# Halves of the memory in other tiles, made beside the last query columns

## The reference

```python
qkv = u @ w_qkv                                  # 16 query heads, 4 key/value heads of 64
q, k, v = split(qkv); q, k = rotary(q), rotary(k)
# each block of 128 rows looks at itself and the block before it, with a sink:
s = where(valid, (q @ k.T) * 64**-0.5, -inf)
p = exp(s - m); o = (p @ v) / (sum(p) + exp(sink - m))
u = o @ w_o
h = h + rms_norm(u, g_mix_post)
# cross attention to a memory of 256 rows, 4 heads of 256:
q = rms_norm(h, g_x_pre) @ w_q
k, v = split(rms_norm(mem, g_mem) @ w_kv)
u = softmax(q @ k.T / 16) @ v @ w_o
```

## Time and profile before

| | |
|---|---|
| median of 3 runs | 3600.88 us (3600.04 to 3605.23) |
| profiled execution | 3602.97 us, its span 3601.2 us |
| PE busy | 3408.3 us (95%) |
| DVE busy | 1788.2 us (50%) |
| ACT busy | 1326.3 us (37%) |
| mean granted TensorE clock | 0.971 of 2.4 GHz |

### The profile page before, as it was taken

One profiled execution on the slowest core, in us unless ns is written; L12 is line 12 of the kernel. 1 busy time (PEld: TensorE's weight loads), 2 busy tenths in 40 slices (PEclk: granted clock), 3 DMA queues, 4 the chain that ended last, 5 costly groups with the idle time before them and its releaser, 6 DMA issues.

```text
span 3601.2 us, 38290 instructions
## 1 busy us (share of the span) xinstructions
PE 3408.3 (95%) x15668; PEld 2798.7 (78%) x15668; DVE 1788.2 (50%) x2679; ACT 1326.3 (37%) x2104; POOL 112.4 (3%) x100
## 2 busy tenths in 40 slices
PE   8999989999999999899999999898999889889998
PEld 6888777888788887778887778667888678667886
DVE  4333685433453347753334764546444764554444
ACT  3222554322232226543223443334332564334321
POOL 0000000000000000000001000000000100000000
PEclk9999999999999999999999999999999999999999
DMA  4332311333233332123332323212333223113332
GB/s 145 100 100 88 76 47 53 106 97 96 82 94 99 99 95 59 42 76 108 97 97 73 88 83 105 70 42 85 95 98 98 60 59 106 53 42 102 97 98 66
DMA packets 604286, 304.10 MB, mean 84 GB/s; under 512 B 43600, under 2 KB 601808, under 8 KB 603984
## 3 DMA queue, kind: packets, MB, share of 16 engines
q1 hardware_dynamic: 604112, 301.66, 29.2%
HBM read 299.52 MB, written 2.10 MB: 84 GB/s over the span
## 4 chain that ended last, share of the span: by engine, by line
PE 80%; DVE 11%; ACT 6%; issue 1%; DMA 1%; SPq 0%; DVEq 0%; ACTq 0%
PE ps L1561 25%; PE ps L1562 24%; PE ps L1569 24%; DVE XR L2044 2%; DVE wl L1948 1%; PE ps L1578 1%; DVE Y L2121 1%; PE ps L1585 1%; PE ps L1718 1%; PE ps L1619 1%; ACT XH L1775 1%; ACT wh L1733 1%; DVE XL L2030 1%; ACT tmp L1795 1%; PE ps L1604 1%
## 5 line engine op out<-in xcount | busy, mean ns | idle before, releaser
L1561 PE MATMUL ps<-XH,wh 128*128 128x512 f32 x2600 | 1056.1, 406 | 78.9 <-ACT XH L1775 33.1
L1569 PE MATMUL ps<-XL,wh 128*128 128x512 f32 (+1 forms) x2856 | 1067.7, 385 | 0.0
L1562 PE MATMUL ps<-XH,wl 128*128 128x512 f32 x2600 | 1028.4, 396 | 0.0
L1948 DVE TENSOR_TENSOR wl<-raw,wh 128x1024 fp32r<-128x1024 f32 (+1 forms) x565 | 680.4, 1210 | 521.3 <-ACT wh L1733 521.1
L1733 ACT ACTIVATE wh<-raw 128x1024 fp32r<-128x1024 f32 (+1 forms) x565 | 583.3, 1039 | 519.4 <-PE ps L1569 492.6
L1561 PEld LDWEIGHTS ps<-XH,wh 128*128 128x128 f32 x2600 | 499.0, 192 | 200.8 <-issue 36.0
L1569 PEld LDWEIGHTS ps<-XL,wh 128*128 128x128 f32 x2856 | 545.4, 191 | 107.3
L1562 PEld LDWEIGHTS ps<-XH,wl 128*128 128x128 f32 x2600 | 499.8, 192 | 103.6 <-issue 2.7
L1561 PE MATMUL ps<-HHa,wh 128*128 128x512 f32 x1088 | 427.0, 392 | 9.2 <-DVE HLa L1952 5.8
L1562 PE MATMUL ps<-HHa,wl 128*128 128x512 f32 x1088 | 423.6, 389 | 0.0
L1569 PE MATMUL ps<-HLa,wh 128*128 128x512 f32 x1088 | 408.0, 389 | 0.0
(11 more groups left out here) (311 smaller groups left out, 3184.5 us busy)
## 6 DMA issues: line engine op xcount, KB each, us to landing
raw<-in_ffn_w_gu SPq DMA_DIRECT2D x176, 512.0 KB, 3.8
raw<-in_w_ff SPq DMA_DIRECT2D x128, 512.0 KB, 4.1
raw<-in_ffn_w_down SPq DMA_DIRECT2D x64, 512.0 KB, 3.9
raw<-in_w_xkv SPq DMA_DIRECT2D x32, 512.0 KB, 3.9
raw<-in_ev_w_in SPq DMA_DIRECT2D x25, 512.0 KB, 3.9
raw<-in_ffn_w_down SPq DMA_DIRECT2D x32, 384.0 KB, 3.4
raw<-in_w_in SPq DMA_DIRECT2D x24, 512.0 KB, 3.9
raw<-in_w_out SPq DMA_DIRECT2D x64, 128.0 KB, 2.7
```

What stands on the lines that cost most here:

```text
L1561: e.matmul(bank[:, 0:n], t.wh[u % SPL][:, k, :], h, start=first, stop=False)
L1562: e.matmul(bank[:, 0:n], t.wl[u % SPL][:, k, :], h, start=False, stop=False)
L1569: m = e.matmul(bank[:, 0:n], t.wh[u % SPL][:, k, :], l, start=False, stop=last)
L1948: self.e.tensor_tensor(wl, raw, f32(wh), ALU.subtract).then_inc(self.s["lo"], self.tag("lo", f"lo.{i}"))
```

## The change

In the second layer of the second block, the memory's halves leave XL. The hi parts go to Y[6], Y[7], HLb[6] and HLb[7] (two of 256 columns in each), which were lent as temporaries before; the lo parts are written over the raw memory in Y[0:4], through a second view of Y in the rounded type, `Yr`. They no longer wait for query 7's last matmul. `normed` and `parts` become one sequence of 17 steps, four of which are issued after each of queries 4 to 7 and the last one behind them; it takes no attention steps along. `swa` lends two tiles in place of six. The tiles of the halves are given on after the last matmul of the memory (`mem.last`) in place of the last subtraction. For the first layer the halves stay in XL and their order is as it was.

```diff
         self.XL = sb("XL", [P, KD, T], F32R)
+        with nc.sbuf_tensor("Yr", [P, KD, T], F32R) as Yr:
+            self.Yr = Yr
         self.Y = sb("Y", [P, KD, T])
...
-        extra = [Y[:, i, :] for i in range(4, 8)] + [M1[:, i, :] for i in (6, 7)]
-        self.lend(extra[:4], yf)
-        self.lend(extra[4:], menter)
-        mem = Memory(self, 1, Y[:, 0:4, :], yf)
+        extra = [Y[:, i, :] for i in (4, 5)]
+        self.lend(extra, yf)
+        mem = Memory(self, 1, Y[:, 0:4, :], [t.Yr[:, 6, :], t.Yr[:, 7, :], t.HLb[:, 6, :], t.HLb[:, 7, :]], (yf, menter))
+        prep = itertools.chain(mem.normed(), mem.parts())
...
         for i in range(4, 8):
             query(i)
-            if i == 4:
-                for _ in mem.normed():
-                    pass
-        for _ in mem.parts():
-            next(self.filler[0], None)
+            for _ in range(4):
+                next(prep, None)
+        for _ in prep:
+            pass
         for i in range(16):
             mem.unit(i)
 
         def finish():
             mem.turn()
             keys = self.reclaim(extra)
-            self.y_free = [self.y_free, keys, mem.raw_done]
-            self.m_leave(done[0], keys)
+            self.y_free = [self.y_free, keys, mem.last]
+            self.m_leave(done[0], keys, mem.last)
...
-    def __init__(self, walk, l, raw, *free):
+    def __init__(self, walk, l, raw, his, free):
...
-        XL = walk.t.XL
-        self.mh = XL[:, 0:4, :].rearrange("p a (b t) -> p (a b) t", b=2)
-        self.ml = XL[:, 4:8, :].rearrange("p a (b t) -> p (a b) t", b=2)
+        XL, w = walk.t.XL, T // 2
+        if his:
+            self.his = [his[k // 2][:, w * (k % 2):w * (k % 2) + w] for k in range(KD)]
+            self.los = [walk.t.Yr[:, k // 2, w * (k % 2):w * (k % 2) + w] for k in range(KD)]
+            self.free = free
+        else:
+            self.his = [XL[:, k // 2, w * (k % 2):w * (k % 2) + w] for k in range(KD)]
+            self.los = [XL[:, 4 + k // 2, w * (k % 2):w * (k % 2) + w] for k in range(KD)]
+            self.free = None
...
-                w.p_mem_hi(f"{self.k}.h{k}", self.mh[:, k, :], self.tile(k), (f"{self.k}.n{k}", w.x_free))
+                free = w.x_free if self.free is None else self.free
+                w.p_mem_hi(f"{self.k}.h{k}", self.his[k], self.tile(k), (f"{self.k}.n{k}", free))
```

More of the change, by code:

```diff
@@ L1 @@
+import itertools
 import math
@@ L1074, in mixer2 @@
         self.tmp.give(rx, lru_state[3])
-        mem = Memory(self, 0, t.XM[:, 4:8, :], self.x_free)
+        mem = Memory(self, 0, t.XM[:, 4:8, :], None, self.x_free)
         extra = [Y[:, i, :] for i in (0, 1, 4, 5)]
@@ L1431, in parts @@
             if k < KD:
-                w.p_mem_hi(f"{self.k}.h{k}", self.mh[:, k, :], self.tile(k), (f"{self.k}.n{k}", w.x_free))
+                free = w.x_free if self.free is None else self.free
+                w.p_mem_hi(f"{self.k}.h{k}", self.his[k], self.tile(k), (f"{self.k}.n{k}", free))
             if k:
                 j = k - 1
-                w.p_mem_lo(f"{self.k}.l{j}", self.ml[:, j, :], self.tile(j), self.mh[:, j, :], f"{self.k}.h{j}")
-                self.ms.append((self.mh[:, j, :], self.ml[:, j, :], f"{self.k}.l{j}"))
+                w.p_mem_lo(f"{self.k}.l{j}", self.los[j], self.tile(j), self.his[j], f"{self.k}.h{j}")
+                self.ms.append((self.his[j], self.los[j], f"{self.k}.l{j}"))
             yield
```

## The result

The changed kernel takes 3607.02 us (median of 20 runs, 3604.02 to 3609.18); the kernel before takes 3601.62 beside it (20 runs). The ratio is 1.0015, with a 95% interval of 1.0008 to 1.0022. It is slower by 5.4 us: within the 0.2% that the prediction called no change, but above its range, whose upper end was 3605.0, and on the other side of zero from the forecast of -2.0. All lines of the changed kernel lie 11 further down than before (L1952 is L1963 now). The page of the profiled execution (3607.99 us) answers to the earlier trace rows: PE has the same instructions, is busy 1.3 us less in a span 5.0 us longer, and so stands idle 6.3 us more.

What follows compares the result with a forecast made beforehand. PE, busy 95% of the span, was taken as the bound, with an ACT-DVE ring under the query columns. Terms -20.5 + 8.3 + 1.1 + 5.7 + 2.0 + 1.4 = -2.0 us gave 3598.9 us, range 3590.5 to 3605.

Steps and rivals of the forecast that it cites:

- nine attention steps: Steps from the removed stretch come later in PE's queue, at 0.92 us each among units: +8.3 us.
- stretch: PE's time between query 7's last transposes and unit 0's first matmul is removed: -20.5 us.
- normed tiles: Eight DVE operations, four now behind query 4's rotary and four behind query 5's, give and take the same 1.6 us: 0.
- three subtractions on the ring: DVE subtractions behind query 6's rotary, in the ACT-DVE ring of waits under the query columns, delay query 7's end: +1.1 us.
- wait in unit 0: PE waits after unit 0's first matmuls for subtraction 3, issued only after query 7's rotary: +5.7 us, bounds 0 and 7.4.
- half clock behind it: After the wait in unit 0, PE runs at half clock for 4 us: +2.0 us, bounds 0 and 2.9.
- last half: Out projection's k = 7 waits for tile 7's second half, made from step 72 directly ahead: +1.4 us, bounds 0 and 2.
- The sign by which it should show: In the changed kernel's profile, query 7's 0.33 us wait of PE becomes about 1.4 us.
- Full cover: Halves all there when unit 0 begins, no wait or half clock: -9.7 us, 3591.2 us; chance 0.18 including most of it.
- Too few temporaries: Tiles given too late make each of eight projected columns wait like the 1.41 us: +11.3, 3610 us; chance 0.14.

Runs made afterwards that it cites:

- e9: Changed kernel with one attention step issued between query 7 and unit 0; 3598.6 us, ratio to the kernel before 0.9990.
- e6: Changed kernel, memory's 16 DVE operations dealt ahead of rotaries of queries 1 to 7, 8 ACT copies behind those of queries 4 and 5; 3599.8 us.
- e7: e6 with one attention step issued between query 7 and unit 0; 3588.9 us (5 runs), ratio to the kernel before 0.9969.
- e5: Changed kernel with four attention steps issued between query 7 and unit 0; 3602.3 us, ratio to the kernel before 1.0001.
- e3: Changed kernel with all 17 preparing steps dealt 6, 6, 5, 0 behind queries 4 to 7; 3603.1 us, ratio to the kernel before 1.0008.
- e11: e7 repeated unchanged; 3591.3 us (6 runs), ratio to the kernel before 0.9968.
- e10: Changed kernel with three attention steps issued between query 7 and unit 0; 3599.0 us, ratio to the kernel before 0.9989.
- e2: Kernel before, with two lent temporaries in place of six and nothing else; 3601.5 us, ratio to the kernel before 1.0004.
- e1: Changed kernel, with units 10, 12 and 14 taking the second free PSUM bank; 3606.1 us, ratio to the kernel before 1.0017.
- e4: Changed kernel with five attention steps issued between query 7 and unit 0; 3602.6 us, ratio to the kernel before 1.0007.
- e8: e6 with three attention steps issued between query 7 and unit 0; 3594.0 us, ratio to the kernel before 0.9980.

## Why the prediction was wrong

**The step that failed** is "Its nine attention steps are not removed. They come later in PE's queue, beside other work." I priced them as nine pieces of PE time and took their order against the units as without effect. The term for them is +8.3. Moving an odd number of steps across unit 0 turned the parity of every step behind it, and with it two things: the order in which ACT and DVE get a head's split and the next unit's weight halves, and which columns take a bank that a split releases. The price is the four waits, 1.44 + 1.63 + 1.50 + 1.37 = 5.9 us. e9 shows that the odd step makes or removes them on the changed kernel, e6 against e7 on another one, and e5 has the waits back at two places. The two effects of the parity were not tested apart. The timelines above show the first (the split ends 4.9 in place of 3.6 us behind the values), and e9's remaining waits for a split, 0.36 us at most, fit it; the share of the second stays open.

**Point by point**, forecast and measured:

| term | forecast | measured |
|---|---|---|
| stretch | -20.5 | -20.8 |
| nine steps, without waits | +8.3 | about +10.5 |
| normed tiles | 0 | 0 |
| three subtractions on the ring | +1.1 | +1.1 |
| wait in unit 0 | +5.7 | +5.7 |
| half clock behind it | +2.0 | +2.0 |
| last half | +1.4 | +1.5 |
| banks released by a split | none | +5.9 |
| at the first scores, other phase of the clock | none | +1.5 |
| sum over the changed stretch | -2.0 | +7.5 |

- *Nine steps.* The units and the out projection take 117.0 us before and 142.6 after (2938.70 to 3055.69, 2921.05 to 3063.68): +25.6, of which 5.7 + 2.0 + 5.9 + 1.5 are waits and clock. The rest is 10.5 us. The sum priced all nine as full steps, 0.92 us each. The out projection without its waits grew by 4.6 us, 0.65 for each of its seven steps; the units without waits and clock grew by 5.9 us for two more steps. Before, the last steps, which have no scores left to make (64 to 72), ran beside the last units; after, 30 of the 32 steps beside the units are full ones, and seven of the nine short ones stand beside the out columns.
- *Ring.* Query 5's 3.51 us became 1.91 and 1.93 as the prediction had it, which gives and takes the same. From the 1.93 us wait to query 7's last matmul it is 12.8 us, from the same transposes at 2905.20 to 2916.92 before it is 11.7: +1.1. The sign by which it should show did not come: query 7's wait was to grow to 1.4 us and is 0.16. The granted clock in 2908 to 2912 was 0.57 (1.00 before); PE at half clock was busy there for a part of what it would have waited.
- *Wait in unit 0.* Both ends of it came 2 us later than in the working (subtraction 3 ends at 2928.03, not 2926.05) and the difference held; ACT's lag behind PE was 2.2 us (2921.05 to 2923.26), forecast 2.0. e3 shows the wait to be owed to the order of the subtractions: with them dealt earlier, it vanishes.
- *Half clock.* The clock term was right. The Trainium skill (TensorE: Matmul & The Clock Gate, Loop structure matters more than you think) shows this order, matmuls that run cold behind a long wait of PE (there a wait for a DMA). The trace agrees with 0.50 behind the 5.72 us. e3, e6 and e11, without the wait, have no such window there.
- *Last half.* 1.50 us at 3033.64, with the reason given: step 72 directly ahead of k = 7. In e9 six steps are left for the out projection in place of seven, step 72 comes one k earlier, and the wait is gone; so e9 wins this one by the count of the steps and not by their parity: e5, with an even count and three steps left, has no such wait either.
- *At the first scores.* In key column 1, PE waits for query 0's rotary in both kernels, 2.95 us until 2833.06 before and 4.58 until 2833.64 after. Up to the end of this wait the changed kernel is 0.5 to 0.6 us behind, as at the first XH matmul; behind it, at the next scores (2834.75 and 2836.70), it is 1.95 behind. Before, the half clock fell ahead of the wait and was hidden by it; after, it fell behind it (0.65 in 2832 to 2836, above) and was paid for. The window of the kernel before:

```profile
2824.00:2828.00 4.00, 4.00 (x14) 3.17 (x13) 1.75 (x3) 3.49 (x6) 0.00 (x0) 0.58 0.84 274
```

Runs with the same code up to there show both: 2.96 us in e5, 4.57 in e9 and e10. So these 1.5 us are not of the change but of the one execution that was profiled, like the 2.3 us that come back behind the changed stretch. Without the 1.5 us, the terms of the change come to +6.0, and the medians differ by 5.4.

**The rivals.** Full cover did not come: the wait is there. Too few temporaries is excluded by e2. The page rule cited for it (the Trainium skill, Perfetto Trace Analysis, Optimization Strategy: a gap that repeats can mean too few buffers) fits the symptom, gaps of 1.4 to 1.6 us at every second unit, in which PE waits for a PSUM bank. In e1 the next bank of the list changed the waits' releaser and not the waits; whether one more bank would have removed them, no run here shows. One moved step removed them without one (e9).

**Open.** Why e5 is not slower than e4, whether the bank or the order on ACT and DVE is what counts in the four waits, and how often each phase of the clock occurs.

## What to carry to other kernels

When filler work is interleaved by a fixed ratio, treat a moved block of it as a shift of phase: before pricing it, list for the new order which first-in first-out buffer each consumer takes, which instruction releases it, and what stands ahead of that instruction on its engine. A wait that repeats with the period of the interleave (here every second unit) is cheap to test by moving one filler step, which was worth 9 us here, 5.9 of them the four waits. Vector work that must go somewhere costs least ahead of an instruction that waits for another engine anyway (here 1.1 us of idle time before a rotary); behind it, three subtractions cost 1.1 us here.

## What the runs showed of the hardware

In the changed kernel, the wait of 1.93 us that ended at 2907.20 was followed by a granted clock of 0.57 over 4 us, while the one of 1.91 us that ended at 2895.04 had 1.00 behind it (2896 to 2900), as had the one of 3.51 us in the kernel before. So the length of the wait alone did not tell whether the clock fell. The same code up to the first scores came with the half clock before PE's wait for query 0's rotary in some executions and behind it in others, and the wait was 2.95 to 2.99 us in the one case (before, e2, e4 to e7, e11) and 4.57 or 4.58 in the other (changed, e1, e3, e8 to e10).
